# Two-layer encoder on one core: other places and another order for the loads and first products of layer 1

## Chip, core and metric

The kernel runs on one core of a Trainium2 chip. The metric is device time in microseconds (us) for one execution of the whole program. The engines are TensorE (PE; its weight loads are shown apart as PEld), VectorE (DVE), ScalarE (ACT), GpSimd (POOL), and SyncE (SP), which here does nothing but issue transfers. Each engine runs its own list of instructions in order and waits on semaphores for the others.

## What is computed

256 tokens of width 2048 in float32 go through two layers. This is the reference, cut to what matters here:

```python
h = x
for layer in range(2):
    hn = rmsnorm(h, norm_mix_g[layer])
    if layer % 2 == 0:
        h = h + attn_mlstm_mixer(hn, ...)
    else:
        h = h + multiscale_pool_mixer(hn, pool_w[0], layer_scale[0])
    h = h + peer_ffn(rmsnorm(h, norm_ffn_g[layer]), peer_wq[layer], peer_keys[layer], peer_u[layer], peer_v[layer])
return rmsnorm(h, norm_f)

def multiscale_pool_mixer(xn, pool_w, layer_scale):
    # four groups of 512 channels, windows 2, 4, 8, 16:
    # pooled[t] = mean(xn[t - w//2 : t + w//2]) - xn[t]   (clipped at the ends)
    y = einsum('bsgc,gcd->bsgd', pooled, pool_w)
    return y * layer_scale

def peer_ffn(xn, w_query, sub_keys, u, v):
    q = xn @ w_query              # 8 heads, 2 halves of 128
    sc = q . sub_keys             # 128 keys for each half
    # top 16 of each half, top 16 of their 256 sums: 16 experts a head, of 16384
    act = gelu(einsum('tkd,td->tk', u[expert], xn))
    return einsum('tk,tkd->td', gate * act, v[expert])   # gate: softmax of the 16 best sums
```

## The kernel before

The 256 tokens are two tiles of 128 tokens, one token on each partition. `h` holds both tiles; `xns[0]` and `xns[1]` hold the normalised tiles, `xnT` their transpose. Nearly everything else lies in one large buffer, `arena`, which is carved anew for each stage; two tiles of the program that lie at the same place there exclude each other in time. `low` is the first four PSUM banks, the other four have names of their own.

**A layer's expert stage.** For each head `queries` multiplies a 2 MB block of `wq` (64 matmul instructions, since each float32 product is two) and `scores` multiplies by the keys. DVE finds the best keys (`route_halves`, `route_pairs`, `route_experts`) and writes the experts' numbers. POOL then gathers for each of the 16 experts of a head one row of `peer_u` for each of 128 tokens (1 MB a gather, `gather_u`, L449) into a ring of six slots for tile 0; a gather into a slot waits until the dot product that read it is done. DVE makes the dot products (`dot`, L1120). One row in four, from the second head of tile 0 on, is done by PE instead. Later come the rows of `peer_v`, half of them gathered (L464, L1146), half streamed and multiplied by PE (L1616).

**The seam between the layers.** When layer 0's last product is added (`add_dense`, L1178), SP issues in this order: the pooling matrix `PM` (`poolm`), the pooling weights `poolw`, the scale `lsB`, the first query block (`load_wq(1, 0)`, L338), the keys, and the gain of the next norm. `wq` has two slots, and block 1 belongs in slot 1. `PM` and `lsB` lie in that slot 1. So SP waits for `h1_ready` to reach 8, which is the last of the additions of `add_pooled` for both tiles, before it issues `load_wq(1, 1)`.

The engines meanwhile: a norm is a sum of squares on ACT (L497), a mean on DVE (L803), a root on ACT (L499), a reciprocal (L805) and a scaling on DVE (L811). Norm 2 makes `xns` for both tiles. The pooling product on PE (L1629) multiplies for each tile `t` and each 128-channel chunk `c` the tile's tokens into all 256 output tokens: `PM[:, c // 4, t]` is 128 x 256. Then PE does `project_pooled(0, g)` (L1555), DVE adds the result (L1185, L1186), norm 3 of tile 0 follows, the transposes (L1281), and `queries` and `scores` of head 0 for tile 0 alone (L1533, L1544). While DVE routes head 0, PE does `project_pooled(1, g)`; after its additions DVE makes two dot products, and then takes its part of norm 3 of tile 1. PE has `queries` for head 1 next, then the transposes of tile 1. ACT copies head 1's queries out of PSUM (`route_q`, L659) and then takes its part of tile 1's norm. DVE copies half of the transposes (L817) after two more dot products. Everything for tile 1 waits for this norm.

The order of all lists is written by hand. The pooling matrix holds 1/count within a window of at most 8 tokens to either side and -1 on the diagonal, so tile 0 (tokens 0 to 127) has entries only in output columns 0 to 135 and tile 1 only in 120 to 255; the rest of it is zeros.

Of the kernel before, what the change touches and what calls it, by code (L numbers as in the profile page):

```python
# [20 lines left out]
P = 128  # L21
D = 2048
TB = 2
S = TB * P
# [31 lines left out]
VD, VG = 1024, D - 1024  # L56
VH = VD // 2
VR, DR = 8, 4
HK = PH * PK
ND, DG = 16, 2  # L60
GROUPS = TB * PH
ROWS = GROUPS * PK
# [1 line left out]
QT = 4  # L64
QUADS = P // QT
W_AT, V_AT, VD_AT, T_AT = 8192, 0, 4096, 40960
POOLW = (2, 4, 8, 16)
ARENA = 41344
OUT_AT = 33152


def hybrid_encoder(nc, x, consts, poolm, w_proj, w_gates, w_out, b_gate, conv_w, q_gain, k_gain,
                   ml_gain, gains, layer_scale, pool_w, wq, keys, pu0, pvg0, pvd0, pu1, pvg1, pvd1, out):
    pu, pvg, pvd = [pu0, pu1], [pvg0, pvg1], [pvd0, pvd1]
    with ExitStack() as ctx:
# [22 lines left out]
        psum = [low[:, i * BANK:(i + 1) * BANK] for i in range(4)]  # L98
# [24 lines left out]
        wqb = carver(W_AT + 2 * KC * P * 2, ARENA)(2, KC, 2 * P)  # L123
# [11 lines left out]
        carve = carver(OUT_AT, T_AT)  # L135
# [41 lines left out]
        goh2 = gB[:, 2 * QT * P:4 * QT * P].rearrange("p (b i n) -> p b i n", b=2, i=QT)  # L177

        poolw = carver(0, W_AT)(4, 4, BANK)
        slot1 = wqb[:, 1].rearrange("p k c -> p (k c)")  # L180
        PM = slot1[:, 0:D].rearrange("p (g t s) -> p g t s", g=4, t=TB)
        lsB = slot1[:, D:2 * D]
        ytmp = eq.rearrange("p q k a -> p (q k a)").rearrange("p (a b) -> p a b", a=2)
        idx_all = sb("idx_all", [P, GROUPS, PK], u32)
        i16 = sb("i16", [P, 4, PK], u32)
# [136 lines left out]
        @block.sync  # L322
        def _(sp):
            def load_half(i, src):

                if i >= WR:
                    sp.wait_ge(*half_read(i - WR))
                sp.dma_start(wslot[i % WR].rearrange("p k c -> p (k c)"), src).then_inc(w_got[i % WR], 16)

            def gain(o):  # L330

                if o:
                    sp.wait_ge(s["xn_ready"], TB * o)
                sp.dma_start(gB[:], gains[o].partition_broadcast(P)).then_inc(s["ld_gain"], 16)

            def load_wq(L, hd):
                slot = hd % 2
                sp.dma_start(wq_slots[slot].rearrange("p k c -> p (k c)"), wq[L, hd]).then_inc(ld_wq[slot], 16)  # L338

            sp.dma_start(h[:, 0, :], x[0:P, :]).then_inc(s["ld_x0"], 16)  # L340
            gain(0)
            sp.dma_start(cst[:], consts).then_inc(s["ld_c"], 16)
            sp.dma_start(h[:, 1, :], x[P:S, :]).then_inc(s["ld_x1"], 16)
            for i in range(2):
                load_half(i, w_proj[i // 2, i % 2])
            sp.dma_start(wg, w_gates.rearrange("p (k c) -> p k c", k=KC)).then_inc(s["ld_small"], 16)
            sp.dma_start(bgB, b_gate.partition_broadcast(P)).then_inc(s["ld_small"], 16)
            sp.dma_start(cvw, conv_w).then_inc(s["ld_small"], 16)
            sp.dma_start(gB_q, q_gain.partition_broadcast(P)).then_inc(s["ld_small"], 16)
            sp.dma_start(gB_k, k_gain.partition_broadcast(P)).then_inc(s["ld_small"], 16)  # L350
            sp.dma_start(mlg, ml_gain.partition_broadcast(P)).then_inc(s["ld_small"], 16)
            for i in range(2, 2 * N_IN):
                load_half(i, w_proj[i // 2, i % 2])
                if i == 4:
                    gain(1)


            for m in range(2 * NO):
                load_half(2 * N_IN + m, w_out[m])
                if m == NO + 1:  # L360

                    sp.wait_ge(s["ymt_ready"], 2 * TB)
                    sp.wait_ge(s["yt_ready"], AU)
                    sp.dma_start(keysT, keys[0].rearrange("p (a n) -> p a n", a=2 * PH)).then_inc(s["ld_keys"], 16)
                    for hd in range(2):
                        load_wq(0, hd)
            sp.wait_ge(s["out_mm"], NO + 1)
            slot, _ = w_half(LAST_HALF)
            sp.dma_start(wslot[slot].rearrange("p k c -> p (k c)"), w_out[NO]).then_inc(w_got[slot], 16)
            def load_vd(L, n):  # L370

                if n >= DR:
                    sp.wait_ge(s["vd_used"], L * (NK - 1) + n - DR + 1)
                else:
                    sp.wait_ge(s["dot_done"], (L + 1) * NDOT)
                sp.dma_start(vdense[:, n % DR], pvd[L][n]).then_inc(vd_got[n % DR], 16)

            for L in range(LAYERS):
                for hd in range(2, PH):

                    sp.wait_ge(s["q_mm"], EVENTS * L + hd + 1)
                    load_wq(L, hd)
                for n in range(NK):
                    load_vd(L, n)
                    if n == 16:

                        sp.wait_ge(s["spread_mm"], TB * QUADS * (L + 1))
                        gain(2 + 2 * L)
                if L == 0:

                    sp.wait_ge(s["dense_done"], 1)
                    sp.wait_ge(s["vacc_done"], NV)
                    sp.dma_start(PM.rearrange("p g t s -> p (g t s)"), poolm).then_inc(s["ld_pm"], 16)
                    sp.dma_start(poolw, pool_w.rearrange("p (g k c) -> p g k c", g=4, k=4)).then_inc(s["ld_pool"], 16)
                    sp.dma_start(lsB, layer_scale.partition_broadcast(P)).then_inc(s["ld_scale"], 16)
                    load_wq(1, 0)
                    sp.dma_start(keysT, keys[1].rearrange("p (a n) -> p a n", a=2 * PH)).then_inc(s["ld_keys"], 16)
                    gain(3)
                    sp.wait_ge(s["h1_ready"], 4 * TB)
                    load_wq(1, 1)  # L400
            for t in range(TB):
                for c in range(2):
                    sp.wait_ge(s["fin_ready"], 2 * t + c + 1)
                    cols = slice(c * D // 2, (c + 1) * D // 2)
                    sp.dma_start(out[t * P:(t + 1) * P, cols], h[:, t, cols]).then_inc(s["out_done"], 16)
            sp.wait_ge(s["out_done"], 16 * 2 * TB)
# [71 lines left out]
        def _(e):  # L478
# [264 lines left out]
            for L in range(LAYERS):  # L743
                if L:
                    norm(2, 0)
                    norm(2, 1)
                    for n in range(0, KC // 2, 2):
                        e.wait_ge(s["pool_mm"], n + 1)
                        activation(xnT[:, 2 * n:2 * n + 2], psum[n][:, :].rearrange("p (a b) -> p a b", a=2), ACT.Copy
                                   ).then_inc(s["pool_act"], 1)  # L750
                norm(1 + 2 * L, 0)
                evac_xt(1 + L, 0)
                route_q(L, 0, 0, 1)
                route_exp(L, 0, 0, 1)
                route_q(L, 1, 0, 1)
                norm(1 + 2 * L, 1)
                evac_xt(1 + L, 1)
                stage_xn(L, 0)
                route_exp(L, 1, 0, 1)
                for ev_ in (2, 3):  # L760
                    route_q(L, ev_, 1, 2)
                    route_exp(L, ev_, 1, 2)
                route_q(L, 4, 0, 2)
                for j in range(1, PH):
                    turn_u(L, 4 * j - 4)
                    turn_u(L, 4 * j - 3)
                    if j + 3 < EVENTS:
                        route_exp(L, j + 3, 0, 2)
                    if j + 4 < EVENTS:
                        route_q(L, j + 4, 0, 2)  # L770
                    turn_u(L, 4 * j - 2)
                    turn_u(L, 4 * j - 1)
                stage_xn(L, 1)
                gelu(L, 0)
                turned(L, 0)
                for q in range(QUADS):
                    one_hots(L, q)
                    if q:
                        spread_out(L, 0, q - 1)
                spread_out(L, 0, QUADS - 1)  # L780
                gelu(L, 1)
                turned(L, 1)
                for q in range(QUADS):
                    if q % (QUADS // ND) == 0:
                        diagonal(L, q // (QUADS // ND))
                    spread_out(L, 1, q)
# [482 lines left out]
        def _(pe):  # L1269
# [350 lines left out]
            for L in range(LAYERS):  # L1620
                if L:
                    pe.wait_ge(s["ld_pm"], 16)
                    pe.wait_ge(s["acc_evac"], 4)
                    for t in range(TB):
                        pe.wait_ge(s["xn_ready"], 4 + t + 1)
                        for n in range(KC // 2):
                            for i in range(2):
                                c = 2 * n + i
                                ins = mm(psum[n][:, i * S:(i + 1) * S], xns[t][:, c * P:(c + 1) * P], PM[:, c // 4, t],  # L1629
                                         start=t == 0 and i == 0, stop=t == 1 and i == 1)  # L1630
                            if t:
                                ins.then_inc(s["pool_mm"], 1)
                    pe.wait_ge(s["ld_pool"], 16)
# [127 lines left out]
```

## Time and profile before

| what | value |
|---|---|
| median of 3 runs | 3136.72 us (3135.51 to 3137.5) |
| profiled execution | 3131.51 us, its span 3129.6 us |
| mean granted PE clock | 0.851 of full speed |
| busy: PE, DVE | 2292.8 us (73%), 2180.1 us (70%) |
| busy: POOL, ACT | 1011.0 us (32%), 677.7 us (22%) |
| read from memory | 1055.24 MB, 338 GB/s over the span |

The profile is one execution. Its span runs from the first instruction to the last; the execution is 1.9 us longer. Where the clock is told, 1.00 is 2.4 GHz and 0.50 is 1.2 GHz, the two levels; a value between them is a stretch with both. A busy PE isn't PE at its peak.

### The profile page before, as it was taken

Reading aid. Unit: us, or ns where it says so; the run is one execution under the profiler, and the core shown is the slowest. Engines: PE = TensorE matmul, PEld = TensorE weight load, DVE = VectorE, ACT = ScalarE, POOL = GpSimd, SP = SyncE. Lnnn points to the kernel's source line nnn. Section 1 sums busy time; section 2 is a strip of 40 time slices with the busy share of each in tenths; the row PEclk is TensorE's granted clock in tenths of the full one; section 3 lists DMA queues with packets and bytes.
Section 4 is the critical chain, followed back from the end, with each engine's and each line's share of the span. In section 5 each row is a group of like instructions: output and inputs, shape, how many; then the busy total and the mean of one; then the engine's idle time right before and its main releaser. Section 6 shows DMA issues by size and latency. Waiting matters only on the chain.

```text
span 3129.6 us, 25966 instructions
## 1 busy us (share of the span) xinstructions
PE 2292.8 (73%) x9248; PEld 1706.4 (55%) x9248; DVE 2180.1 (70%) x3263; ACT 677.7 (22%) x1645; POOL 1011.0 (32%) x1028
## 2 busy tenths in 40 slices
PE   8999999588853400999999575888533109999994
PEld 4685545587743300766666344878533006666662
DVE  1341113988979999856666739889899998566667
ACT  1241111122229910200000011222289203000000
POOL 0000000432333333344544414233333333445444
PEclk9999999799975555999999787999855559999997
DMA  5423243989989999699999948899999996999998
GB/s 212 153 111 135 108 169 152 414 332 404 378 364 422 421 422 413 214 410 409 409 409 409 378 182 334 332 406 380 377 421 421 421 420 209 410 409 409 409 409 337
DMA packets 194528, 1059.08 MB, mean 338 GB/s; under 512 B 21856, under 2 KB 22240, under 8 KB 121312
## 3 DMA queue, kind: packets, MB, share of 16 engines
q0 software_dynamic: 147456, 805.37, 63.7%
q1 hardware_dynamic: 46944, 252.06, 20.3%
q8 instruction: 74, 1.21, 0.2%
q14 instruction: 54, 0.44, 0.0%
HBM read 1055.24 MB, written 2.10 MB: 338 GB/s over the span
## 4 chain that ended last, share of the span: by engine, by line
DMA 48%; PE 23%; DVE 22%; issue 3%; POOL 3%; ACT 1%; DVEq 0%; SPq 0%; ACTq 0%; POOLq 0%
DMA arena<-pu,idx_all 23%; DMA xnT<-pvg,idx_all 13%; DMA arena<-pvg,idx_all 11%; DVE arena L1120 10%; PE bank L1293 6%; DVE h L1146 4%; PE bank L1378 3%; PE bank L1599 2%; PE bank L1607 2%; PE low L1498 2%; PE bank L1533 1%; POOL arena L449 1%; PE low L1487 1%; PE low L1555 1%; PE bank L1487 1%
## 5 line engine op out<-in xcount | busy, mean ns | idle before, releaser
L1120 DVE CUSTOM_DVE_ANT_0 arena<-arena,low 128x2048 f32<-128x2048 f32 x420 | 954.2, 2286 | 125.1 <-DMA arena<-pu,idx_all 123.5
L449 POOL DMA_INDIRECT arena<-pu,idx_all x456 | 453.8, 995 | 1467.5 <-DVE idx_all L1094 767.3
L1616 PE MATMUL low<-arena 128*128 128x512 f32 x2048 | 879.6, 592 | 0.1
L1616 PEld LDWEIGHTS low<-arena 128*128 128x128 f32 x2048 | 604.7, 295 | 274.8 <-DMA arena<-pvd 1.0
L1146 DVE SCALAR_TENSOR_TENSOR h<-arena,cst,h 128x1024 f32<-128x1024 f32 x240 | 307.9, 1285 | 164.5 <-DMA arena<-pvg,idx_all 157.4
L1146 DVE SCALAR_TENSOR_TENSOR h<-xnT,cst,h 128x1024 f32<-128x1024 f32 x240 | 307.6, 1285 | 157.9 <-DMA xnT<-pvg,idx_all 150.9
L464 POOL DMA_INDIRECT arena<-pvg,idx_all x256 | 252.3, 986 | 296.8 <-DVE h L1146 215.7
L464 POOL DMA_INDIRECT xnT<-pvg,idx_all x256 | 250.3, 978 | 283.7 <-DVE h L1146 215.8
L1599 PE MATMUL bank<-arena 128*128 128x128 f32 x512 | 132.8, 441 | 201.6 <-ACT arena L728 201.6
L1533 PE MATMUL bank<-xnT,arena 128*128 128x256 f32 (+1 forms) x1280 | 239.2, 351 | 19.2 <-DMA arena<-wq 13.3
L1567 PE MATMUL bank<-xnT,arena 128*128 128x128 f32 x1792 | 247.6, 289 | 1.7 <-ACT arena L692 0.9
L497 ACT ACTIVATE arena<-h 128x2048 f32<-128x2048 f32 x10 | 19.1, 1905 | 1022.8 <-DVE h L1178 944.9
L1533 PEld LDWEIGHTS bank<-xnT,arena 128*128 128x128 f32 x1280 | 214.7, 203 | 42.0 <-DMA arena<-wq 14.1
L1567 PEld LDWEIGHTS bank<-xnT,arena 128*128 128x128 f32 x1792 | 233.1, 204 | 2.4 <-ACT arena L692 1.3
L1599 PEld LDWEIGHTS bank<-arena 128*128 128x128 f32 x512 | 114.0, 327 | 220.6 <-ACT arena L728 220.6
L1588 PE MATMUL bank<-cst,arena 128*128 128x128 f32 x8 | 2.8, 447 | 309.0 <-DVE cst L1135 309.0
L1293 PE MATMUL bank<-arena,xnT 128*128 128x512 f32 x448 | 198.7, 599 | 2.0 <-issue 1.6
L692 ACT ACTIVATE arena<-bank 128x512 f32<-128x512 f32 x224 | 133.8, 597 | 304.4 <-PE bank L1574 289.1
L1588 PEld LDWEIGHTS bank<-cst,arena 128*128 128x128 f32 x8 | 1.2, 204 | 310.0 <-DVE cst L1135 310.0
L1574 PE MATMUL bank<-cst,arena 128*128 128x128 f32 x608 | 103.3, 297 | 79.3 <-DVE cst L1129 25.8
L719 ACT ACTIVATE arena<-cst,arena 128x128 f32<-128x128 f32 x512 | 155.8, 389 | 0.1
L1293 PEld LDWEIGHTS bank<-arena,xnT 128*128 128x128 f32 x448 | 84.3, 192 | 101.8 <-issue 99.8
(222 smaller groups left out, 2218.8 us busy)
## 6 DMA issues: line engine op xcount, KB each, us to landing
arena<-pvd SPq DMA_DIRECT2D x256, 512.0 KB
arena<-w_proj SPq DMA_DIRECT2D x22, 2048.0 KB, 7.5
arena<-wq SPq DMA_DIRECT2D x16, 2048.0 KB
arena<-w_out SPq DMA_DIRECT2D x9, 2048.0 KB, 7.9
arena<-pu,idx_all POOLq DMA_INDIRECT x494, 14.8
gB<-gains SPq DMA_DIRECT2D x5, 1024.0 KB, 10.1
xnT<-pvg,idx_all POOLq DMA_INDIRECT x256
arena<-pvg,idx_all POOLq DMA_INDIRECT x256
```

What stands on the lines that cost most here:

```text
L449: nc.gpsimd.indirect_dma_start(U[t][slot], None, pu[L], bass.IndirectOffsetOnAxis(row(n), 0)).then_inc(u_got[t][slot], 16)
L464: nc.gpsimd.indirect_dma_start(vslots[m % VR], None, pvg[L], bass.IndirectOffsetOnAxis(idx_all[:, t * PH + hk // PK, hk % PK:hk % PK + 1], ...
L692: activation(UXT[i % 2][:, 4 * b:4 * b + 4], psum[4][:, :].rearrange("p (a b) -> p a b", a=4), ACT.Copy).then_inc(s["ux_ev"], 1)
L719: ins = activation(oh[:, b, i], iota, ACT.Square, scale=-1.0, bias=sT[:, x, t:t + 1])
L1120: vec.tensor_tensor_reduce(out=u, in0=u, in1=low[:, :] if staged else xns[t], scale=1.0, scalar=0.0, op0=ALU.mult, op1=ALU.add, accum_out= ...
L1146: vec.scalar_tensor_tensor(acc, vslots[m % VR], wv[:, t, hk:hk + 1], acc, ALU.mult, ALU.add).then_inc(s["vacc_done"], 1)
L1293: ins = mm(psum[4 + t][:, :], xnT[:, HALF * hf + k, t * P:(t + 1) * P], wslot[slot][:, k], start=hf == 0 and k == 0, stop=hf == 1 and k == ...
L1533: ins = mm(psum[6][:, p_ * S + t0 * P:p_ * S + t1 * P], wq_slots[slot][:, k, p_ * P:(p_ + 1) * P], xnT[:, k, t0 * P:t1 * P], start=k == 0, ...
L1567: ins = mm(psum[5][:, i % 4 * P:(i % 4 + 1) * P], UXT[i % 2][:, c], xnT[:, c, 0:P], start=c == 0, stop=c == KC - 1)
L1574: ins = tr(psum[4][:, x * P:(x + 1) * P], UX[i % UP][:, (4 * b + x) * P:(4 * b + x + 1) * P], ident)
L1599: ins = mm(psum[4 + q % 2][:, i * P:(i + 1) * P], o1[:, q % 2, i], o2[:, q % 2, i], start=True, stop=True)
L1616: ins = mm(psum[2 * t + c][:, 0:VH], W[t][:, :, n], vdense[:, n % DR, c * VH:(c + 1) * VH], start=n == 0, stop=n == NK - 1)
```

## The change

There are five edits, all at the seam.

1. `PM` and `lsB` are carved at another place in `arena`, behind `xns[1]`.
2. `load_wq(1, 1)` no longer waits for `h1_ready`. It is issued right behind the keys and ahead of the gain.
3. On ACT, in layer 1 only, the norm of tile 1 stands ahead of `route_q` of head 1.
4. The pooling product of tile 0 covers columns 0 to 135.
5. That of tile 1 covers columns 120 to 135 and 136 to 255, as two matmuls, of 16 and of 120 columns.

```diff
+BANDS = (((0, P + max(POOLW) // 2),), ((P - max(POOLW) // 2, P + max(POOLW) // 2), (P + max(POOLW) // 2, S)))
...
-        slot1 = wqb[:, 1].rearrange("p k c -> p (k c)")
-        PM = slot1[:, 0:D].rearrange("p (g t s) -> p g t s", g=4, t=TB)
-        lsB = slot1[:, D:2 * D]
+        carve = carver(OUT_AT + D, T_AT)
+        PM = carve(4, TB, S)
+        lsB = carve(D)
...
                     load_wq(1, 0)
                     sp.dma_start(keysT, keys[1].rearrange("p (a n) -> p a n", a=2 * PH)).then_inc(s["ld_keys"], 16)
+                    load_wq(1, 1)
                     gain(3)
-                    sp.wait_ge(s["h1_ready"], 4 * TB)
-                    load_wq(1, 1)
...
-                route_q(L, 1, 0, 1)
-                norm(1 + 2 * L, 1)
+                if L:
+                    norm(1 + 2 * L, 1)
+                    route_q(L, 1, 0, 1)
+                else:
+                    route_q(L, 1, 0, 1)
+                    norm(1 + 2 * L, 1)
...
-                                ins = mm(psum[n][:, i * S:(i + 1) * S], xns[t][:, c * P:(c + 1) * P], PM[:, c // 4, t],
-                                         start=t == 0 and i == 0, stop=t == 1 and i == 1)
+                                for lo, hi in BANDS[t]:
+                                    ins = mm(psum[n][:, i * S + lo:i * S + hi], xns[t][:, c * P:(c + 1) * P],
+                                             PM[:, c // 4, t, lo:hi], start=t == 0 and i == 0, stop=i == 1 and hi == S)
```

SP's list at the seam, before and then after. A bracket tells what a row waits for.

```order
L393 DMA arena<-poolm 128x2048 [waits vacc_done,dense_done]
L394 DMA arena<-pool_w 128x8192
L395 DMA arena<-layer_scale 128x2048
L338 DMA arena<-wq 128x4096
L397 DMA arena<-keys 128x2048
L334 DMA gB<-gains 128x2048 [waits xn_ready]
L338 DMA arena<-wq 128x4096 [waits h1_ready]
```

```order
L394 DMA arena<-poolm 128x2048 [waits vacc_done,dense_done]
L395 DMA arena<-pool_w 128x8192
L396 DMA arena<-layer_scale 128x2048
L339 DMA arena<-wq 128x4096
L398 DMA arena<-keys 128x2048
L339 DMA arena<-wq 128x4096
L335 DMA gB<-gains 128x2048 [waits xn_ready]
```

The second query block has lost its wait, and stands ahead of the gain.

ACT's list in layer 1, where tile 1's norm comes; `bank6` holds the queries of head 1.

```order
 L665 ACTIVATE cst<-cst 128x16 [waits bd_ready]
-L659 ACTIVATE arena<-bank6 128x2x128 [waits q_mm]
 L497 ACTIVATE arena,stat<-h 128x2048 [waits pool_mm,h1_ready]
 L499 ACT_TABLE_LOAD
 L499 ACTIVATE stat<-stat 128x1 [waits ms_done]
+L659 ACTIVATE arena<-bank6 128x2x128 [waits q_mm]
 L505 ACTIVATE xnT<-low 128x4x128 [waits tp_done] x2
```

The square, the table load and the root now stand ahead of the copy of the queries.

## Rows read from the trace of the kernel before

**Rows 1.** The page: shares by engine in the chain that ended last.
```profile
DMA 48%; PE 23%; DVE 22%; issue 3%; POOL 3%; ACT 1%; DVEq 0%; SPq 0%; ACTq 0%; POOLq 0%
```

**Rows 2.** The chain of waits at the seam: start us, length us, what.
```profile
1789.65 6.68 PE low L1629 x16
1796.32 3.45 PE bank L1629 x16
...
1806.68 13.75 PE low L1555 x32
...
1855.07 11.74 DMA arena<-wq
...
1866.85 9.29 PE bank L1533 x64
...
1880.18 2.35 DVE arena L811
```

**Rows 3.** SP's timeline: when a transfer was issued.
```profile
1792.41 0.33 SPq L334 DMA_DIRECT2D gB<-gains  x1
1855.07 100.00 SPq L338 DMA_DIRECT2D arena<-wq  x4
```

**Rows 4.** DVE's timeline at tile 1's norm and ahead of it; idle time in brackets.
```profile
1824.01 0.15 DVE L803 TENSOR_SCALAR stat<-stat 128x1 f32<-128x1 f32 x1 [2.14 <-ACT arena L497]
...
1824.63 2.35 DVE L811 SCALAR_TENSOR_TENSOR arena<-h,stat,gB 128x2048 f32<-128x2048 f32 x1
...
1858.04 2.29 DVE L1120 CUSTOM_DVE_ANT_0 arena<-arena 128x2048 f32<-128x2048 f32 x1 [0.61 <-DMA arena<-pu,idx_all]
...
1878.47 0.15 DVE L803 TENSOR_SCALAR stat<-stat 128x1 f32<-128x1 f32 x1 [18.13 <-ACT arena L497]
```

**Rows 5.** PE's timeline: the two query products of tile 0, 64 instructions each.
```profile
1831.28 7.38 PE L1533 MATMUL bank<-xnT,arena 128*128 128x128 f32 x64 [0.94 <-ACT xnT L505]
...
1866.85 9.27 PE L1533 MATMUL bank<-xnT,arena 128*128 128x128 f32 x64 [13.27 <-DMA arena<-wq]
```

**Rows 6.** PE's timeline and line 1313's durations (min/median/max ns): 16-column products in layer 0.
```profile
35.67 8.59 PE L1313 MATMUL bank<-arena,xnT 128*128 128x16 f32 x64
...
L1313 PE MATMUL bank<-arena,xnT x64: 179/263/376, 35.7 to 43.9; 128*128 128x16 f32 x64
```

**Rows 7.** Stretches of 1 us: length, busy us of PE, PEld, DVE, ACT, POOL, PEclk, DMA share, GB/s.
```profile
41.00:42.00 1.00, 1.00 (x8) 1.00 (x7) 0.00 (x0) 0.00 (x0) 0.00 (x0) 0.62 1.06 442
48.00:49.00 1.00, 1.00 (x3) 0.38 (x2) 0.35 (x4) 0.00 (x0) 0.00 (x0) 0.97 0.00 0
1795.00:1796.00 1.00, 1.00 (x5) 0.82 (x4) 0.00 (x0) 0.00 (x0) 0.00 (x0) 0.65 0.91 393
```

**Rows 8.** Transfers between 1735 and 1960 us: line, count, KB each, median us to landing.
```profile
arena<-pool_w SPq DMA_DIRECT2D x1, 4096.0 KB, 14.4
arena<-layer_scale SPq DMA_DIRECT2D x1, 1024.0 KB, 16.4
...
gB<-gains SPq DMA_DIRECT2D x1, 1024.0 KB, 18.6
```

**Rows 9.** ACT's timeline at tile 1's norm.
```profile
1876.44 1.90 ACT L497 ACTIVATE arena<-h 128x2048 f32<-128x2048 f32 x1
...
1878.45 1.28 ACT L499 ACT_TABLE_LOAD   x1
```

**Rows 10.** POOL's timeline: first and ninth gather of layer 1.
```profile
1848.78 0.94 POOL L449 DMA_INDIRECT arena<-pu,idx_all  x1 [75.52 <-DVE idx_all L1094]
...
1885.01 2.75 POOL L449 DMA_INDIRECT arena<-pu,idx_all  x1 [22.62 <-DVE cst L1120]
```

**Rows 11.** DVE's timeline: ninth and seventeenth dot product of layer 1.
```profile
1900.17 2.29 DVE L1120 CUSTOM_DVE_ANT_0 arena<-arena 128x2048 f32<-128x2048 f32 x1
...
1923.97 2.29 DVE L1120 CUSTOM_DVE_ANT_0 arena<-arena,low 128x2048 f32<-128x2048 f32 x1 [0.23 <-DMA arena<-pu,idx_all]
```

**Rows 12.** Longer stretches, columns as in Rows 7.
```profile
1880.00:1925.00 45.00, 22.85 (x148) 22.10 (x148) 44.22 (x70) 5.13 (x9) 22.86 (x13) 0.73 0.75 291
...
2325.00:2575.00 250.00, 49.39 (x192) 42.31 (x191) 229.83 (x201) 118.72 (x347) 94.38 (x101) 0.50 1.01 422
```

More of the change, by code:

```diff
@@ L58 @@
 VR, DR = 8, 4
+POOLW = (2, 4, 8, 16)
 HK = PH * PK
+BANDS = (((0, P + max(POOLW) // 2),), ((P - max(POOLW) // 2, P + max(POOLW) // 2), (P + max(POOLW) // 2, S)))
 ND, DG = 16, 2
@@ L66 @@
 W_AT, V_AT, VD_AT, T_AT = 8192, 0, 4096, 40960
-POOLW = (2, 4, 8, 16)
 ARENA = 41344
```

## Prediction, made before the changed kernel was run

> **What bounds the kernel now.** I read the page's chain first. Over the whole span it is mostly transfers [rows 1], but the change touches only some 100 us between the layers, and a share over 3130 us tells nothing of those. So the chain of waits at the seam comes next [rows 2]. There the end is passed from the pooling product (from 1789.65) to its projection (1806.68), over tile 0's norm and first queries, to a transfer of `wq` from 1855.07, then to the queries that read it (1866.85) and to tile 1's norm, whose scaling starts at 1880.18. The transfer is not long because of its bytes alone: SP issued it only at 1855.07 [rows 3], when the last pooled addition was done. The timelines show who stood still. PE was idle 13.27 us ahead of its queries [rows 5], DVE 18.13 us ahead of tile 1's norm [rows 4], POOL 22.62 us ahead of its ninth gather, because DVE had freed no slot [rows 10]. From then to 1925 DVE was busy 44.22 us of 45, so DVE sets the pace and time gained on it is kept [rows 12].
>
> **The pooling product.** Before, 64 instructions of 256 columns took 1789.65 to 1806.68, 17.0 us. The first 16 took 6.68 us and the next 16 3.45 [rows 2], for the clock was at half speed until about 1795.7 [rows 7]. At full clock 256 columns cost 3.45/16 = 0.216 us and 128 columns 7.38/64 = 0.115 [rows 5], so a column costs (0.216 - 0.115)/128 = 0.0008 and 136 columns 0.122. The 16-column products of layer 0 took 8.59 us for 64, with the clock falling at about 41.6, 5.9 us in [rows 6, 7]: at r each at full clock and 2r after, 5.9/r + 2.7/2r = 64, r = 0.113. A narrow matmul is thus as dear as one of 128 columns, and 120 columns lie between, 0.113 too.
> Tile 0 has 32 instructions of 136 columns: in the 6.0 us of half clock 24.6 of them at 0.244, the other 7.4 at 0.122, 0.9 us; 6.9 us in all. Tile 1 has 32 pairs, 64 instructions at 0.113, 7.2 us, where 32 of 256 columns took 6.9. Sum 14.1, **gain 2.9 us**, all from tile 0. The bounds: all at full clock 32 x 0.122 + 7.2 = 11.1, gain 5.9; all at half clock 22.3, a loss of 5.3. I take 2.9, because PE starts at the same moment after the same idle as before.
> What the rows say of 16 columns agrees with a rule: the Trainium skill ("TensorE: Matmul & The Clock Gate", section "LDWEIGHTS (loading the stationary operand)") lets a load of 128 weight columns take 107 ns whatever the product's width. The same page's section "Back-to-back issue gap" gives a lone matmul of 16 columns some 25 ns and one of 120 about 52; by that tile 1 would be 2.5 us (an estimate from that page) and the gain 7.6. The row is against that, and my sum doesn't use it.
>
> **The later gain and the early query block.** `wq` block 1 adds 2 MB ahead of the gain in the queue, at 422 GB/s [rows 12] 5.0 us. The gain landed at 1792.41 + 18.6 = 1811.0 [rows 3, 8], now 1816.0. Tile 0's scaling, its first reader, was at 1824.63 [rows 4] and is to be at 1821.7: hidden, with 5.7 us to spare. Past that margin each us would count. The pooling weights (14.4 us after issue) and the scale (16.4) [rows 8] stand ahead in the queue and don't move; the projection starts at 1803.8, some 7 us after its weights.
>
> **The wait that goes.** All up to the last pooled addition moves up by 2.9, to 1852.2. PE's 13.27 us of idleness go, and so does the half clock behind it: 9.27 us of queries against 7.38 [rows 5]. PE's next queries then run 1850.7 to 1858.1. They alone are worth 15.2 us to PE.
>
> **ACT's new order.** Before, ACT copied the queries (done by PE at 1876.14) and only then squared; the scaling came 4.0 us after PE was done [rows 2, 9]. Now square (1.90) and table load (1.28) run from 1852.2 and are over by 1855.7, with the reads between. What is late next is DVE itself: it has two dot products ahead of tile 1's mean, the second waiting a little for its gather, ending at 1858.04 + 2.29 = 1860.33 before [rows 4], now 1857.4. From a mean to the scaling are 0.62 us when ACT is free (1824.01 to 1824.63) [rows 4]. So the scaling starts at 1858.0 instead of 1880.18: **22.1 us, of which 2.9 are the product and 19.2 the two waits** (1880.18 - 1860.33 - 0.62). With edit 2 alone the scaling would follow the queries' end, 1858.1 + 4.0 = 1862.1; so edit 3 is worth 4.1 of them.
> Queued behind the root on ACT is now the copy of head 1's queries. The root waits for DVE's two dot products, until 1857.9; the queries are ready at 1858.1. It costs nothing; if a gather is late it delays scores that DVE doesn't read before its ninth dot product. On PE, the transposes of tile 1 wait for the scaling (1860.4) as before, and DVE first has two more dot products, 4.4 us, over them.
> The second query block no longer shares the queues with the first gathers. That is a gain of at most the 0.61 us that DVE waited [rows 4]; I take none. The new place in memory costs nothing: no row has an operation for it.
>
> **Whether DVE's lead is kept.** A gather is 128 rows of 8 KB, 1.05 MB, 2.5 us at 422 GB/s. The first is issued at 1848.78 - 2.9 = 1845.9 [rows 10]; nine take 22.4 us from 1847.1, to 1869.5, and the ninth is wanted at 1900.17 - 22.1 = 1878.1 [rows 11]. Nothing runs dry. At the 291 GB/s of the stretch from 1880 to 1925 [rows 12] (a rate of what was asked for, not of what was possible) sixteen gathers would take 57.7 us, to 1904.8, where DVE would want the last near 1921.5 - 22.1 = 1899.4: a loss of 5.4 us at most. After that the list is as before, each gather tied to a dot product, so the lead goes through to the end. Sum: 3131.51 - 22.1 = 3109.4 for the profiled execution; it was 5.2 below the median, and against the median 3136.7 - 22.1 = **3114.6**.
>
> **Rivals.**
> *The clock stays low (faster still).* PE was busy 1.00 of the time with 16-column products when the clock fell to half [rows 6, 7], and tile 1's product has 68 columns an instruction. If the clock doesn't rise in the product, it takes 22.3 us, 8.2 more than forecast; layer 0's clock came back after 6.4 us of 512-column products [rows 7], at half speed another 3.2 lost. 22.1 - 11.4 = 10.7 left: 3126.0, or 3122.8 with the first part alone. For it: that row. Against it: 68 columns are far from 16. The Trainium skill (same page, section "Part 1: The HAM clock gate (the "warmup" mystery)") has the gate follow how busy PE has been; by that a PE busy without a gap keeps full clock, my forecast, but the trace disagrees, with PE busy 1.00 at the fall to 0.62.
> *The gathers set the pace.* The 5.4 us above: 3120.0. Against it: the ninth gather has 8.6 us in hand.
> *Slower: narrow products don't overlap.* If each of the 96 instructions takes its whole 0.376 us, the longest of the 16-column ones [rows 6], the product is 36.1 us, 19.1 more than before and all of the 19.2 of the waits; with 3.2 for the clock afterwards 3139.8, and with the projection wholly at half clock (13.75 more [rows 2]) 3150.4. It decides from a product of 36.2 us. Against it: 64 of them took 8.59 us, not 24.
> *No effect.* The chain at the seam isn't what sets DVE's work, 3136.7. Against it: the 18.13 us of idleness.
>
> **How the numbers follow.** Forecast 0.75, low clock 0.13, gathers 0.05, narrow products 0.03, no effect 0.04. A measurement of this kernel tells 0.2% (6.3 us) from no change. The first three are faster by more: 0.93. Same 0.04, slower 0.03. The range goes from 3114.6 less the 3.0 of a product at full clock, the 0.6 and some 3 for run to run (3135.51 to 3137.5 before), 3108, to 3125, which takes in the gathers and most of the low clock and leaves out less than 2 in 10.
>
> **What would show it.** Right: the two query blocks issued within a few us; the product at some 14 us; PE's idle gap ahead of head 1's queries gone; DVE's 18 us wait under 1; ACT's square right behind the last pooled addition. Wrong: a product over 20 us with PEclk 0.50 to its end, a wait of tile 0's scaling for the gain, or waits of dot products for gathers before the seventeenth.

## The result, and the profile after

| | before | after |
|---|---|---|
| median | 3136.11 us (3131.77 to 3137.5, 4 runs) | 3113.31 us (3112.24 to 3115.55, 4 runs) |
| profiled execution | 3131.51, span 3129.6 | 3115.55, span 3113.8 |

The ratio is 0.9931, with a 95% interval of 0.9913 to 0.9948: 22.8 us faster by the medians, with 3114.6 predicted. A second series gave 3114.79 us against 3136.05 (0.9922, 0.991 to 0.9935). The two profiled spans differ by 15.8 us only: the profiled execution of before was 4.6 us under its median, that of the changed kernel 2.2 us over its own. Where in the trace these 7 us lie is asked below.

The chain of waits of the changed kernel at the seam (start us, length us, what), to hold against [rows 2]; the code stands four or five lines lower:

```profile
1789.38 3.97 PE low L1634 x16
1793.35 2.82 PE bank L1634 x16
1796.17 3.56 PE low L1634 x32
1799.73 3.57 PE bank L1634 x32
1803.31 13.76 PE low L1559 x32
...
1828.32 9.51 PE bank L1537 x64
...
1849.17 8.07 DMA arena<-pu,idx_all
1857.27 2.29 DVE arena L1124
...
1860.10 2.35 DVE arena L815
```

The transfer of `wq` is gone from it. The pooling product has two rows for tile 0 (6.8 us) and two for tile 1 (7.1 us), and tile 1's scaling (L815) starts at 1860.10 where it started at 1880.18. What it follows now are a gather and the second dot product of tile 0.

SP's timeline and the landing of the gain (issued at 1792.14, 22.9 us to landing), to hold against [rows 3, 8]:

```profile
1784.58 0.47 SPq L339 DMA_DIRECT2D arena<-wq  x1
1792.14 0.33 SPq L335 DMA_DIRECT2D gB<-gains  x1
```

```profile
gB<-gains SPq DMA_DIRECT2D x1, 1024.0 KB, 22.9
```

PE's timeline: transposes of tile 0, its first queries, and the queries of head 1, to hold against [rows 5]:

```profile
1823.67 3.68 PE L1285 MATMUL bank<-cst,arena 128*128 128x128 f32 x16 [6.62 <-DVE arena L815]
1828.32 9.49 PE L1537 MATMUL bank<-xnT,arena 128*128 128x128 f32 x64 [0.97 <-issue]
...
1852.57 7.31 PE L1537 MATMUL bank<-xnT,arena 128*128 128x128 f32 x64
```

The last row has no bracket: head 1's queries follow the projection without a gap, where PE had been idle 13.27 us. But the first queries took 9.49 us where they took 7.38 before. One stretch of 1 us shows why; PEclk is the third number from the end:

```profile
1832.00:1833.00 1.00, 1.00 (x8) 1.00 (x7) 0.00 (x0) 0.00 (x0) 0.00 (x0) 0.63 0.00 0
```

The clock rose only there, 4 us into the queries. In the first profile of before they ran wholly at full clock.

ACT and DVE at tile 1's norm, to hold against [rows 4, 9]:

```profile
1854.22 1.91 ACT L497 ACTIVATE arena<-h 128x2048 f32<-128x2048 f32 x1 [9.20 <-DVE h L1190]
...
1856.24 1.28 ACT L499 ACT_TABLE_LOAD   x1
1859.67 0.20 ACT L499 ACTIVATE stat<-stat 128x1 f32<-128x1 f32 x1 [2.14 <-DVE stat L807]
1859.91 0.38 ACT L659 ACTIVATE arena<-bank 128x256 f32<-128x256 f32 x1
```

```profile
1853.49 0.69 DVE L1190 TENSOR_TENSOR h<-h,arena 128x512 f32<-128x512 f32 x1
...
1857.27 2.29 DVE L1124 CUSTOM_DVE_ANT_0 arena<-arena 128x2048 f32<-128x2048 f32 x1 [0.69 <-DMA arena<-pu,idx_all]
...
1859.48 0.15 DVE L807 TENSOR_SCALAR stat<-stat 128x1 f32<-128x1 f32 x1
1859.90 0.16 DVE L809 RECIPROCAL stat<-stat 128x1 f32<-128x1 f32 x1 [0.27 <-ACT stat L499]
1860.10 2.35 DVE L815 SCALAR_TENSOR_TENSOR arena<-h,stat,gB 128x2048 f32<-128x2048 f32 x1
...
1867.99 2.31 DVE L1124 CUSTOM_DVE_ANT_0 arena<-arena 128x2048 f32<-128x2048 f32 x1
```

The first of these rows is the last pooled addition, the last is the fifth dot product. The mean (L807) has no idle time before it, where DVE had waited 18.13 us; square and table load were over at 1857.52, and ACT waited for DVE (2.14 us), not the other way. The copy of head 1's queries (L659) comes right behind the root.

Two rows on what came of DVE's lead, POOL's ninth gather and DVE's first wait for data after the norm, to hold against [rows 10, 11]:

```profile
1864.93 2.75 POOL L449 DMA_INDIRECT arena<-pu,idx_all  x1 [1.67 <-DVE cst L1124]
```

```profile
1909.77 2.29 DVE L1124 CUSTOM_DVE_ANT_0 arena<-arena,low 128x2048 f32<-128x2048 f32 x1 [3.89 <-DMA arena<-pu,idx_all]
```

POOL's 22.62 us of idleness became 1.67. The DMA view of this gather alone (window 1864.92 to 1865.23) has its time to landing:

```profile
arena<-pu,idx_all POOLq DMA_INDIRECT x1, 10.3
```

So it landed at 1875.2. DVE waits for a gather only at its eighteenth dot product, which waits for its experts' numbers and did so before.

### The profile page after: what moved, and what is told of

It reads as the page before. It is cut to its first block, busy times and chain, and to the rows that moved or that the text cites. A ratio compares the mean times of both kernels' runs of the same rounds, so it can differ in the third digit from the quotient of the medians.

```text
span 3113.8 us, 26030 instructions
## 1 busy us (share of the span) xinstructions
PE 2287.6 (73%) x9280; PEld 1706.5 (55%) x9280; DVE 2180.5 (70%) x3263; ACT 677.9 (22%) x1645; POOL 1007.0 (32%) x1028
## 4 chain that ended last, share of the span: by engine, by line
DMA 49%; PE 23%; DVE 22%; issue 3%; POOL 2%; ACT 1%; DVEq 0%; SPq 0%; ACTq 0%; POOLq 0%
DMA arena<-pu,idx_all 24%; DMA xnT<-pvg,idx_all 24%; DVE arena L1124 9%; PE bank L1297 6%; DVE h L1150 4%; PE bank L1382 3%; PE bank L1603 2%; PE bank L1611 2%; PE low L1502 2%; PE bank L1537 1%; DMA arena<-pvg,idx_all 1%; POOL arena L449 1%; PE low L1491 1%; PE bank L1491 1%; PE bank L1571 1%
## 6 DMA issues: line engine op xcount, KB each, us to landing
xnT<-pvg,idx_all POOLq DMA_INDIRECT x256, 14.6
arena<-pvg,idx_all POOLq DMA_INDIRECT x256, 14.6
```

## The experiments

Unless said otherwise each kernel was timed in 5 to 11 executions beside the kernel before (median of before 3135.59 us for the first four experiments, 3136.05 for the next four). The executions differ by 5 us and more from one to the next, so the traces decide and the times confirm. Already the start of the pooling product lies between 1789.4 and 1794.4 us in the profiles, before anything that differs. So all moments are told from that start, and this table collects them. "Product" is its length up to the start of the projection. "Last addition" is the start of the last pooled addition (L1186 before); the last two columns are from it to tile 1's scaling and to the fifth dot product. The two rows of before that go with [rows 4] are the last addition and the fifth dot product:

```profile
1854.35 0.69 DVE L1186 TENSOR_TENSOR h<-h,arena 128x512 f32<-128x512 f32 x1
...
1888.07 2.31 DVE L1120 CUSTOM_DVE_ANT_0 arena<-arena 128x2048 f32<-128x2048 f32 x1
```

| kernel | product | transposes, first queries | last addition | to scaling | to 5th dot product |
|---|---|---|---|---|---|
| before | 16.9 | 3.30, 7.38 | 64.7 | 25.8 | 33.7 |
| before, second profile | 16.6 | 3.67, 9.62 | 67.0 | 26.1 | 34.0 |
| changed | 13.8 | 3.68, 9.49 | 64.1 | 6.6 | 14.5 |
| changed, second profile | 12.4 | 3.67, 7.38 | 60.6 | 6.6 | 14.5 |
| changed, wide product | 16.8 | 3.27, 7.38 | 64.6 | 6.4 | 14.2 |
| changed, ACT's old order | 13.6 | 3.68, 9.44 | 63.9 | 10.4 | 18.3 |
| changed, load late | 13.9 | 3.67, 9.58 | 64.3 | 7.1 | 25.8 |
| changed, PE kept busy | 10.9 | 1.97, 7.38 | 57.4 | 6.8 | 14.6 |
| the same, wide product | 13.9 | 1.97, 7.38 | 60.4 | 6.6 | 14.5 |
| before, narrow product | 13.8 | 3.67, 9.54 | 64.2 | 26.1 | 34.0 |
| before, ACT's new order | 16.7 | 3.68, 9.67 | 67.2 | 6.2 | 25.6 |

**The wide product in the changed kernel.** Theory: the narrow product brings the 2.9 us of the prediction. Rival, from the first profile after: the clock takes them back.

```diff
-                                for lo, hi in BANDS[t]:
-                                    ins = mm(psum[n][:, i * S + lo:i * S + hi], xns[t][:, c * P:(c + 1) * P],
-                                             PM[:, c // 4, t, lo:hi], start=t == 0 and i == 0, stop=i == 1 and hi == S)
+                                ins = mm(psum[n][:, i * S:(i + 1) * S], xns[t][:, c * P:(c + 1) * P], PM[:, c // 4, t],
+                                         start=t == 0 and i == 0, stop=t == 1 and i == 1)
```

> The changed kernel with the pooling product at its old 256 columns (edits 4 and 5 undone). My theory: the narrow product is worth 2.9 us on PE (14 against 17 us), so the time is some 3 us above the changed kernel's 3113.3: 3116. Rival, from the profile of the changed kernel, where the transposes and the first queries of tile 0 ran wholly at half clock (3.68 and 9.49 us against 3.30 and 7.38 before): the clock takes most of it back, the narrow product is worth some 0.5 us, and the time is 3113.8. In the trace the theory has tile 1's scaling some 3 us later than the changed kernel's 1860.1, the rival under 1 us later.

3116.33 us (ratio to before 0.9936, 0.9923 to 0.995). PE's timeline of this kernel:

```profile
1794.13 6.61 PE L1633 MATMUL low<-arena 128*128 128x256 f32 x16 [38.48 <-DVE arena L815]
...
1831.45 3.27 PE L1285 MATMUL bank<-cst,arena 128*128 128x128 f32 x16 [6.62 <-DVE arena L815]
1835.67 7.38 PE L1537 MATMUL bank<-xnT,arena 128*128 128x128 f32 x64 [0.94 <-ACT xnT L505]
```

The product cost 3.0 us more, and transposes and queries 2.5 less, so the scaling came only 0.2 us later than in the changed kernel (71.0 against 70.7). By the trace of this pair the rival holds; the median is what the theory had (3116). Whether the narrow product causes the late clock or only met with it, one pair doesn't tell.

**ACT's old order in the changed kernel.**

```diff
-                if L:
-                    norm(1 + 2 * L, 1)
-                    route_q(L, 1, 0, 1)
-                else:
-                    route_q(L, 1, 0, 1)
-                    norm(1 + 2 * L, 1)
+                route_q(L, 1, 0, 1)
+                norm(1 + 2 * L, 1)
```

> The changed kernel with ACT's old order (edit 3 undone): square of tile 1 behind the copy of head 1's queries. Theory: the scaling of tile 1 comes 4 us behind the end of the queries (1859.9 + 4.0 = 1863.9 instead of 1860.1), the time is 4 us higher, 3117.3. Rival: DVE has other work in the meantime and the order is worth under 1 us, 3113 to 3114.

3118.05 us (0.9941, 0.9928 to 0.9955). DVE's timeline:

```profile
1863.02 0.15 DVE L803 TENSOR_SCALAR stat<-stat 128x1 f32<-128x1 f32 x1 [2.53 <-ACT arena L497]
1864.54 0.16 DVE L805 RECIPROCAL stat<-stat 128x1 f32<-128x1 f32 x1 [1.36 <-ACT stat L499]
```

DVE waits twice, for the square and for the table load, and the scaling comes 10.4 us behind the last addition instead of 6.6: the order is worth 3.8 us, as expected (4).

**The load late in the changed kernel.**

```diff
-                    load_wq(1, 1)
                     gain(3)
+                    sp.wait_ge(s["h1_ready"], 4 * TB)
+                    load_wq(1, 1)
```

> The changed kernel with the wait ahead of the second query block put back (the block issued after the last pooled addition and behind the gain). Theory: ACT's new order lets tile 1's scaling start near 1860 all the same, but PE's queries for head 1 end only near 1874, the transposes of tile 1 stand behind them, and DVE's copy of these comes near 1878 instead of 1867: some 10.5 us lost, 3124. Rival A: all 19 us of the two waits hang on the load, 3132. Rival B: DVE takes nothing from the transposes so early, 3114.

3128.06 us (0.9975, 0.9965 to 0.9985). PE's timeline, then DVE's:

```profile
1871.40 9.30 PE L1538 MATMUL bank<-xnT,arena 128*128 128x128 f32 x64 [13.67 <-DMA arena<-wq]
```

```profile
1872.63 2.29 DVE L1125 CUSTOM_DVE_ANT_0 arena<-arena 128x2048 f32<-128x2048 f32 x1 [2.46 <-DMA arena<-pu,idx_all]
...
1882.79 0.69 DVE L822 COPY xnT<-low 128x512 f32<-128x512 f32 x1 [7.86 <-PE low L1286]
```

The scaling hardly moves (7.1), so the load doesn't hold the norm, and rival A falls. But PE has the queries ahead of the transposes, and DVE waits for these 7.86 us after its fourth dot product. The fifth comes 11.3 us later than in the changed kernel; 10.5 were expected. The 2.46 us for a gather I put down to the late block sharing the queues: ACT's order alone, below, has 2.44 us at the same place with the block as late, the kernels with the early block none. The median is 4 us over the 3124 expected and as far from rival A's 3132; the trace accounts for 11.3 of the 13 to 15 us that it lies above the changed kernel.

**PE kept busy.** Products of the identity, 128 columns wide, in PE's two idle stretches; the bank that they write is overwritten afterwards. They are no part of what is computed.

```diff
                 if L:
+                    pe.wait_ge(s["vacc_done"], NV - 4)
+                    for _i in range(36):
+                        mm(psum[5][:, 0:P], ident, ident, start=True, stop=True)
                     pe.wait_ge(s["ld_pm"], 16)
...
                     for g in range(4):
                         project_pooled(0, g)
+                    for _i in range(24):
+                        mm(psum[5][:, 0:P], ident, ident, start=True, stop=True)
```

> The changed kernel with unneeded 128-column products of the identity on PE in its two idle stretches (72 instructions from four gathered rows before the end of layer 0's additions, 48 between the first projection and tile 0's transposes), which add nothing to the output. Theory: the clock is at full speed when the pooling product starts (11 us instead of 13.9) and at tile 0's transposes and queries (some 2.6 us less): 5.5 us less than the changed kernel, 3107.8. Rival A: only the product gains, 3 us. Rival B: the added products run over into the pooling product or the transposes and give it back: 3113 or more.

3111.2 us (0.9915, 0.9901 to 0.993). PE's timeline:

```profile
1794.40 2.09 PE L1637 MATMUL low<-arena 128*128 128x136 f32 x16 [1.96 <-DVE arena L815]
1796.33 2.02 PE L1637 MATMUL bank<-arena 128*128 128x136 f32 x16
...
1825.85 1.97 PE L1285 MATMUL bank<-cst,arena 128*128 128x128 f32 x16 [1.27 <-DVE arena L815]
1828.76 7.38 PE L1537 MATMUL bank<-xnT,arena 128*128 128x128 f32 x64 [0.94 <-ACT xnT L505]
```

The first 16 instructions of 136 columns take 2.09 us instead of 3.97, the transposes 1.97 instead of 3.68. The last addition comes 6.7 us earlier than in the changed kernel's first profile and 3.2 earlier than in its second; expected were 5.5. The time of 3107.8 that was expected was not reached. Only its sister below has a lower median. It is 3.6 us under the changed kernel of the second series and 2.1 under that of the first, on spreads of 10 us: the seam is shorter by the trace, but the times alone don't prove it faster than the changed kernel.

**The changed kernel again, and the wide product with PE kept busy.** The diff of the second is the two above together.

> The changed kernel again, beside the others on one chip. Both theories: 3113 +- 2 us, tile 1's scaling 70.7 us behind the start of the pooling product as in its first profile. What is asked: whether the transposes and first queries of tile 0 run at half clock again (3.7 and 9.5 us), as they did with the narrow product in three executions out of three.

> The kernel of the unneeded products with the pooling product at its old 256 columns. With PE at full clock all along, the clock can't give back what the narrow product saves. If the clock took the 2.9 us (the reading of the wide product's run), the wide product now costs its full price: 13.8 instead of 11.0 us, tile 1's scaling 2.8 us later behind the start of the product (67.0 against 64.2 us), and the time 2.8 us above the run with the narrow product. Rival, that the narrow product is worth nothing for another reason on the path behind it: the scaling at 64.2 again.

The second profile of the changed kernel, PE's timeline:

```profile
1793.63 3.54 PE L1634 MATMUL low<-arena 128*128 128x136 f32 x16 [38.26 <-DVE arena L815]
1797.01 2.02 PE L1634 MATMUL bank<-arena 128*128 128x136 f32 x16
...
1826.53 3.67 PE L1285 MATMUL bank<-cst,arena 128*128 128x128 f32 x16 [6.62 <-DVE arena L815]
1831.14 7.38 PE L1537 MATMUL bank<-xnT,arena 128*128 128x128 f32 x64 [0.94 <-issue]
```

This misses what I had expected. The clock rose within the first 16 instructions, and the queries ran at full clock. The same kernel reached its last addition at 60.6 us instead of 64.1. So the late clock is not bound to the narrow product.

With PE kept busy (wide product: 3110.81 us, 0.9918, 0.9906 to 0.9931), the clock has no part:

```profile
1792.12 3.69 PE L1636 MATMUL low<-arena 128*128 128x256 f32 x16 [2.36 <-DVE arena L815]
1795.65 3.62 PE L1636 MATMUL bank<-arena 128*128 128x256 f32 x16
```

The scaling stands at 67.0 us behind the start of the product against 64.2 with the narrow one: 2.8 us, nearly all of the 3.0 that the widths cost at full clock (13.9 against 10.9 for the product). What follows on the path keeps it. The medians don't resolve this (3110.81 against 3111.2).

**Edits 4 and 5 alone, and edit 3 alone, on the kernel before.** The diffs are those of the change.

> The kernel before with edits 4 and 5 alone (narrow product, wait and order kept). Clock theory: the product takes 14 us, the transposes and queries of tile 0 run at half clock, and the second query block is issued some 65.0 us behind the start of the product, against 65.4 before: no difference that can be measured, 3135.5. My prediction's term: 2.9 us earlier, 62.5 us behind it, 3132.7.

> The kernel before with edit 3 alone (ACT's order, wait and wide product kept). Theory: the scaling of tile 1 follows the second dot product (71.3 us behind the start of the product instead of 90.5), but head 1's queries end at 86.5 as before, and the transposes stand behind them on PE: copied by DVE at some 89 instead of 97.2, so 8 us gained, 3127.5. Rival A: the whole 19 us come from ACT's order, 3116. Rival B: nothing without the early load, 3135.6.

The narrow product alone: 3133.66 us (0.9991, 0.9982 to 1.0), 2.4 us under before, at the edge of what can be told, and between the clock theory (3135.5) and my term (3132.7), so the time doesn't choose. In its profile the transposes ran at half clock and the queries began at it, and the last addition comes 0.5 us earlier than in the first profile of before and 2.8 earlier than in the second.

ACT's order alone: 3130.58 us (0.9981, 0.9972 to 0.9991), 5.5 us under before; 8 were expected. DVE's timeline:

```profile
1866.89 2.35 DVE L815 SCALAR_TENSOR_TENSOR arena<-h,stat,gB 128x2048 f32<-128x2048 f32 x1
...
1884.79 0.69 DVE L821 COPY xnT<-low 128x512 f32<-128x512 f32 x1 [8.60 <-PE low L1285]
```

From the last addition to the fifth dot product it takes 25.6 us instead of 33.7 or 34.0: 8.1 to 8.5 gained, in line with the expectation. The last addition itself came 2.5 us late by the clock in this execution (67.2 against 64.7). Neither rival holds.

**Sixteen columns.** A single profiled execution, for the rival of the low clock:

```diff
+BANDS = tuple(tuple((lo, min(lo + 16, S if t else P + 8)) for lo in range(P - 8 if t else 0, S if t else P + 8, 16)) for t in range(2))
...
-                                             PM[:, c // 4, t, lo:hi], start=t == 0 and i == 0, stop=i == 1 and hi == S)
+                                             PM[:, c // 4, t, lo:hi], start=t == 0 and i == 0 and lo == 0, stop=i == 1 and hi == S)
```

> The changed kernel with the pooling product cut into pieces of 16 columns (9 for each tile, chunk and pass; 576 instructions, the last piece of each row 8 columns wide), to see the rival of the low clock by itself. If narrow products leave PE at full clock, 576 x 0.113 = 65 us, with 6 us at the start at half clock 68. If the clock goes down to half during them, as in layer 0 after 5.9 us, 576 x 0.226 = 130 us, less what is at full clock in between: 120 to 130. Theory (from layer 0's rows): the second. The profile then says whether 16 columns and the real band product (68 columns on average) differ.

3223.73 us. The product and a stretch of the projection (length, busy us of PE, PEld, DVE, ACT, POOL, PEclk, DMA share, GB/s):

```profile
1796.00:1914.00 118.00, 118.00 (x555) 118.00 (x554) 2.07 (x3) 2.39 (x4) 0.00 (x0) 0.50 0.17 72
1918.00:1922.00 4.00, 4.00 (x10) 1.74 (x10) 1.38 (x2) 0.00 (x0) 0.00 (x0) 1.00 0.00 0
```

The product took 122.9 us (120 to 130 expected). PE was busy in all of 118 us of it and the clock stayed at half; it rose within the first 512-column products. The band product, half of whose instructions for tile 1 have 16 columns and half 120, kept full clock, once it had risen, in all six profiles that have it.

**The kernel before again.** A single profiled execution, for the 7 us between the spans and the medians:

> The kernel before, unchanged, for a second profile. From the 103rd to the 150th dot product of layer 1 its first profile needs 112.5 us, the changed kernel's 115.9 and six of the other seven profiles 115.0 to 116. Theory: the first profile of before was a lucky one there, and this one has some 115.5; then the 3 us that the changed kernel's profile seemed to lose behind the seam are no effect of the change. Rival: 112.5 again, so an earlier start of layer 1's gathers costs 3 us at the change from tile 0 to tile 1.

(The count in it is of all such DVE instructions, 256, of which 28 are sums that PE made and DVE picks out.) It was 3137.91 us, span 3136.1. From the 103rd to the 150th it took 115.8 us, so the 112.5 of the first profile were luck; 115.5 in the narrow product alone and 115.3 in ACT's order alone say the same, and in the profiles of the table none but the first is under 113.7. The 7 us, then, are mostly two draws: 3.3 us here, and some 2 us of the clock at the seam, where the first profile of before had the early rise and that of the changed kernel the late one. PE's timeline:

```profile
1829.67 3.67 PE L1281 MATMUL bank<-cst,arena 128*128 128x128 f32 x16 [6.62 <-DVE arena L811]
1834.28 9.62 PE L1533 MATMUL bank<-xnT,arena 128*128 128x128 f32 x64 [0.94 <-issue]
```

And with the wide product of the kernel before, the transposes ran at half clock and the queries began at it too. So both products have been seen with the early and the late clock. With PE left idle the queries came late to full clock in four of five profiles with the narrow product and in two of four with the wide one. That is too few to say that the product's length has no part in it; it doesn't fix it.

## Why the prediction was right, point by point

**The two waits, 19.2 us: shown.** From the last addition to the scaling it was 25.8 us before and is 6.6, a difference of 19.2. At the fifth dot product it is still 19.2, with the second profile of before 19.5. The parts: edit 3 alone gives 8.1, edit 2 on top of it 11.1 to 11.3; in the other order edit 2 gives 15.4 (33.7 against 18.3) and edit 3 on top 3.8, where the text had 15.2 and 4.1. Their gains overlap, 23.5 us as a sum of each alone against 19.2 together, and neither has the whole: with either alone tile 1 still waits for head 1's queries, on ACT in one case and on PE in the other.

**The pooling product, 2.9 us: right on the average, wrong as the sum of one execution.** The rows' prices held within some 7%, the largest error being 16 columns at full clock (0.106 us measured below, 0.113 in the sum): 64 instructions of tile 1 took 7.1 us (7.2 forecast), the product 13.8 in the table's measure and 13.9 in the chain's, which the forecast used (14.1). The step that failed was that nothing else of the seam changes its clock. When the clock rises, in the product and again in transposes and queries, differs from one execution to the next, by up to 1.4 us in the product (13.8 and 12.4 for the same kernel) and 2.6 in transposes and queries together (10.7 and 13.3 for the kernel before). The first profiles of before and after drew the early and the late case, and showed 0.6 us at the last addition. The mean of the last addition is 63.4 us over five profiles with the narrow product (64.1, 60.6, 63.9, 64.3, 64.2) and 65.9 over four with the wide one (64.7, 67.0, 64.6, 67.2), PE left idle in both: 2.5 us. Within either group the profiles lie up to 3.7 us apart and the groups overlap, so this mean alone is weak evidence for 2.9. The firmer figure is the pair with PE kept busy, one profile each, where it is 2.8 to 3.0. That the seam as a whole comes out near the 22.1 us forecast in the medians is thus right in its mechanism, and a matter of averaging in this term: for the profiled execution the forecast was 3109.4 us, and it took 3115.55.

**The gain behind the query block: hidden, shown.** It landed 1792.14 + 22.9 = 1815.0 (1816.0 forecast), ahead of its reader at 1821.27.

**The lead is kept: mostly shown.** The ninth gather was issued after 1.67 us of waiting for a slot, and from the third dot product on none waited for data before the eighteenth. In the first profiles the shift falls from 20.1 us at the third dot product to 17.1 at the last, most of it around the change from tile 0 to tile 1; the second profile of before takes that part (3.3 us) out. From the fifth dot product to the end of the span I read 1241.5 and 1242.5 us in the two profiles of before, 1245.8 and 1244.3 in the two of the changed kernel: some 2 to 3 us that a start 19 us earlier may cost there, or may not, since the kernel with PE kept busy, with the same seam behind the addition, needs 1240.5, its sister 1241.8 and the wide product 1243.1, while the kernel with the load late, whose fifth dot product comes 11 us later, needs 1246.0. This stays open. The medians show no such loss: 19.2 + 2.5 = 21.7, and they differ by 22.8 in one series and by 21.3 in the other.

**The rivals.** The low clock is shown not to come from the band product (full clock to its end in six profiles), though the mechanism exists: 118 us of 16-column products at half clock. The product took 13.8 us, so narrow products overlap, and the slower rival fell. The gathers didn't set the pace, but they had less in hand than was worked out. The sum had nine of them landed at 1869.5, 8.6 us ahead of use; it left out that the ninth waits for a slot until the third dot product has ended. It was issued at 1864.93 and landed at 1875.2, 4.9 us ahead of its dot product at 1880.10. The eighth, issued at 1860.67 and 12.1 us under way, had 1.9 us. The low clock's price was misread too: the 6.4 us "of 512-column products" in layer 0 run from the fall at 41.6, but those products only start at 44.10, so they had 4.0 us of the low clock and the rival's second loss would be 2.0 us, not 3.2:

```profile
44.10 15.95 PE L1293 MATMUL bank<-arena,xnT 128*128 128x512 f32 x32
```

The range of 3108 to 3125 was wide for the product's clock; single runs of the changed kernel lay between 3105.3 and 3117.8.

## What to carry to other kernels

When two engines each wait for the same late transfer, removing its wait and reordering one engine's list don't add up: here 15.4 and 8.1 us alone, 19.2 together, and neither alone had the whole. Read, for each engine, what stands ahead of the work that others wait for, and price each edit with and without the other. Ask why a load is late; here the cause was two tensors of 1 MB kept in its slot, while other memory was free. A ring of slots also sets when the later gathers start, so a sum of bytes alone gives them too much time in hand. Where PE starts from idleness, two executions of one kernel can differ by a few us (60.6 and 64.1 here), so measure a saving of that size with PE kept busy, or over several profiles.

## What the runs showed of the hardware

With sixteen columns PE was busy 118.00 of 118.00 us and ran at 1.2 GHz from the first to the last. The Trainium skill ("TensorE: Matmul & The Clock Gate", section "Part 1: The HAM clock gate (the "warmup" mystery)") lets the clock follow how busy PE has been; the trace disagrees in that stretch. In the band product the clock, once up, stayed at 2.4 GHz: PEclk was 1.00 over the 7.1 us of tile 1 in all six profiles. Unneeded products ahead of a stretch were enough to have it at 2.4 GHz from the start: 2.09 us instead of 3.97 for the first 16 instructions of 136 columns.

In the run with sixteen columns 144 instructions took 30.7 us, 0.213 each at half clock. At full clock the 16-column products of layer 0 took 5.00/47 = 0.106 us:

```profile
36.00:41.00 5.00, 5.00 (x47) 5.00 (x46) 0.00 (x0) 0.00 (x0) 0.00 (x0) 1.00 0.84 308
```

The pairs of 16 and 120 columns took 3.57/32 = 0.112. PEld was busy for as long as PE, so I read the weight load as the price; no run varies it. The Trainium skill ("TensorE: Matmul & The Clock Gate", section "LDWEIGHTS (loading the stationary operand)") has a rule that gives 107 ns for 128 weight columns, an estimate from that page. The rows at full clock agree; those at half clock have twice that.
